# Two products side by side where TensorE first reads a fresh activation, in a two-layer hybrid diffusion block

## What is computed

```python
def reference(x, c, ctx, ...):
    for i in range(DEPTH):                      # DEPTH = 2
        sh1, sc1, g1, sh2, sc2, g2 = split(silu(c) @ ada_w[i] + ada_b[i], 6)
        h = modulate(rmsnorm(x, norm1_g[i]), sh1, sc1)
        # one input projection h @ w_in: SSD, short convolution, latent attention, Fourier, gates
        merged = sum(sigmoid(gate[k]) * (branch[k] @ w_branch[k]) for k in range(4))
        x = x + g1 * (merged @ w_out[i])
        h = modulate(rmsnorm(x, norm2_g[i]), sh2, sc2)
        x = x + g2 * (square(relu(h @ mlp_w1[i])) @ mlp_w2[i])
    return rmsnorm(x_latent, final_norm_g)
```

## Time and profile before

| what | us |
|---|---|
| median of 3 runs (lowest, highest) | 3272.09 (3267.53, 3280.63) |
| the profiled execution, first to last instruction | 3278.3 |
| TensorE matmul busy in it | 2998.9 (91%) |
| DVE, POOL, ACT busy in it | 1713.4 (52%), 875.8 (27%), 859.5 (26%) |
| TensorE idle, ended by `h_lo` on DVE | 66.3 in 23 waits |
| mean granted TensorE clock | 0.937 of full speed |

### The profile page before, as it was taken

One profiled execution on the slowest core, in us unless ns is written; L12 is line 12 of the kernel. 1 busy time (PEld: TensorE's weight loads), 2 busy tenths in 40 slices (PEclk: granted clock), 3 DMA queues, 4 the chain that ended last, 5 costly groups with the idle time before them and its releaser, 6 DMA issues. The chain is left out here.

```text
span 3278.3 us, 35493 instructions
## 1 busy us (share of the span) xinstructions
PE 2998.9 (91%) x14825; PEld 2420.8 (74%) x14825; DVE 1713.4 (52%) x1815; ACT 859.5 (26%) x1117; POOL 875.8 (27%) x412
## 2 busy tenths in 40 slices
PE   6898899999989899699999996889999988979998
PEld 5764588887878788578787885546877876768886
DVE  3464454543775575787777875641421664241123
ACT  1244311121122222212111222442222222332222
POOL 0210023321223222222222222202432242434442
PEclk6899999999997899899999998999999988989998
DMA  5400042331310033133333332102342201423331
GB/s 146 119 26 1 13 109 78 84 109 39 103 52 1 20 97 116 40 90 99 100 90 92 101 103 76 43 0 58 97 116 58 71 14 44 130 71 93 93 97 64
DMA packets 422264, 242.21 MB, mean 74 GB/s; under 512 B 20284, under 2 KB 418140, under 8 KB 421468
## 3 DMA queue, kind: packets, MB, share of 16 engines
q1 hardware_dynamic: 417388, 216.59, 24.1%
q10 hardware_dynamic: 4240, 23.27, 1.8%
q0 software_dynamic: 480, 0.10, 0.1%
HBM read 231.54 MB, written 8.39 MB: 73 GB/s over the span
## 5 line engine op out<-in xcount | busy, mean ns | idle before, releaser
L893 POOL TENSOR_TENSOR w_lo<-raw,w_hi 128x1024 fp32r<-128x1024 f32 x318 | 778.7, 2449 | 2233.7 <-ACT w_hi L915 2233.7
L426 PE MATMUL slot<-h_hi,w_hi 128*128 128x256 f32 (+1 forms) x2632 | 797.4, 361 | 67.2 <-DVE h_lo L1260 66.3
L426 PE MATMUL slot<-h_lo,w_hi 128*128 128x256 f32 (+1 forms) x2632 | 785.2, 357 | 0.0
L426 PE MATMUL slot<-h_hi,w_lo 128*128 128x256 f32 (+1 forms) x2632 | 784.6, 356 | 0.0
L426 PEld LDWEIGHTS slot<-h_hi,w_hi 128*128 128x128 f32 x2632 | 498.1, 192 | 154.4 <-issue 64.9
L915 ACT ACTIVATE w_hi<-raw 128x1024 fp32r<-128x1024 f32 x318 | 336.0, 1057 | 906.8 <-PE slot L426 532.5
L426 PEld LDWEIGHTS slot<-h_lo,w_hi 128*128 128x128 f32 x2632 | 505.4, 192 | 72.2 <-issue 0.5
L426 PEld LDWEIGHTS slot<-h_hi,w_lo 128*128 128x128 f32 x2632 | 504.3, 192 | 72.4
L1304 DVE TENSOR_REDUCE ksum<-prod 128x128 f32<-128x1024 f32 x160 | 318.9, 1993 | 5.5
L1257 DVE TENSOR_TENSOR prod<-raw,silc 128x1024 f32<-128x1024 f32 x160 | 278.0, 1738 | 2.8
L426 PE MATMUL slot<-f_hi,w_hi 128*128 128x512 f32 (+1 forms) x768 | 238.1, 364 | 16.2 <-DVE f_lo L1260 16.2
(11 more groups left out here) (254 smaller groups left out, 3328.9 us busy)
## 6 DMA issues: line engine op xcount, KB each, us to landing
raw<-in_w_in_dram SPq DMA_DIRECT2D x130, 512.0 KB, 3.9
raw<-in_mlp_w_dram SPq DMA_DIRECT2D x128, 512.0 KB, 4.0
raw<-in_ada_w_dram SPq DMA_DIRECT2D x96, 512.0 KB, 5.1
raw<-in_w_branch_dram SPq DMA_DIRECT2D x32, 512.0 KB, 3.5
raw<-in_w_out_dram SPq DMA_DIRECT2D x16, 512.0 KB, 3.7
x_spill<-x ACTq DMA_DIRECT2D x2, 3072.0 KB, 8.7
x<-x_spill ACTq DMA_DIRECT2D x2, 3072.0 KB, 10.8
dft<-in_dft_dram ACTq DMA_DIRECT2D x2, 2048.0 KB, 10.2
```

The lines of the kernel that those rows point to most:

```text
L426: last = pe.matmul(o[:, c0:c0 + nt], w[:, k, col:col + P], a[:, k, t0:t0 + nt], start=(k == rows[0] and n == 0), stop=(k == rows[-1] and n ...
L893: pool.tensor_tensor(w_lo[:, place[s] % 2, :], raw[:, s % NRAW, :], w_hi[:, place[s] % 2, :].bitcast(F32), ALU.subtract).then_inc(*does("w ...
```

## The change

A new function `product_pair` makes two products together. It takes two PSUM slots and waits for both weight tiles; then, for each contraction tile, it waits for the activation and issues the 6 (or 3) matmuls of the first product and those of the second. It replaces the first two products after each norm of a layer and at the output projection, six pairs in the whole kernel. In `w1` of layer 0 the two `ada_sum` of these products now stand behind the pair.

```diff
+            def product_pair(keys, a_hi, a_lo, sp, ready):
+
+                outs = [take(key) for key in keys]
+                both = [weights(key, key) for key in keys]
+                for k in range(KD):
+                    ready(k)
+                    for o, (wh, wl) in zip(outs, both):
+                        for n, (w, a) in enumerate(((wh, a_hi), (wh, a_lo), (wl, a_hi))):
+                            for c0, t0, nt in sp:
+                                last = pe.matmul(o[:, c0:c0 + nt], w[:, k, 0:P], a[:, k, t0:t0 + nt],
+                                                 start=(k == 0 and n == 0), stop=(k == KD - 1 and n == 2))
+                        if k == KD - 1:
+                            last.then_inc(slot_full, 1)
...
-                for f in range(2):
-                    product((L, "kva", f), (L, "kva", f), KD, 0, h_hi, h_lo, ALL,
-                            (lambda k: pe.wait_ge(*when("h_lo", (L, 1, k)))) if f == 0 else None)
+                product_pair([(L, "kva", f) for f in range(2)], h_hi, h_lo, ALL,
+                             lambda k: pe.wait_ge(*when("h_lo", (L, 1, k))))
...
-                for f in range(KD):
-                    product((L, "out", f), (L, "out", f), KD, 0, h_hi, h_lo, spans(L),
-                            (lambda k: pe.wait_ge(*when("merged_lo", (L, k)))) if f == 0 else None)
+                product_pair([(L, "out", f) for f in range(2)], h_hi, h_lo, spans(L),
+                             lambda k: pe.wait_ge(*when("merged_lo", (L, k))))
+                for f in range(2, KD):
+                    product((L, "out", f), (L, "out", f), KD, 0, h_hi, h_lo, spans(L))
                 mean_of_x((L, "ms", 2), spans(L))
                 for c in range(4):
-                    for f in range(KD):
-                        product((L, "w1", c, f), (L, "w1", c, f), KD, 0, h_hi, h_lo, spans(L),
-                                (lambda k: pe.wait_ge(*when("h_lo", (L, 2, k)))) if c == f == 0 else None)
+                    if c == 0:
+                        product_pair([(L, "w1", c, f) for f in range(2)], h_hi, h_lo, spans(L),
+                             lambda k: pe.wait_ge(*when("h_lo", (L, 2, k))))
+                        for f in range(2):
+                            ada_sum((L, "w1", c, f))
+                    for f in range(0 if c else 2, KD):
+                        product((L, "w1", c, f), (L, "w1", c, f), KD, 0, h_hi, h_lo, spans(L))
                         ada_sum((L, "w1", c, f))
```

## The result

The changed kernel took 3307.4 us (median of 4 runs, 3301.38 to 3315.7), the kernel before, run beside it, 3276.4 (4 runs, 3267.53 to 3284.57): 31 us more by the medians; the ratio is 1.0111 (36 us), 95% interval 1.0076 to 1.0145 (25 to 48 us). The same kernel run again later beside 29 runs of before: 3300.3 against 3271.5, 29 us more; 1.0080 (1.0056 to 1.0104, 18 to 34 us). The forecast was 25 us more and 3297, with a range of its own of 3288 to 3304 and a wide one of 3284 to 3308: the measured time lies above the first. The sign and the place of the loss held.

A forecast was written before the change was run, and what follows sets the result against it. TensorE, busy 91% of the span, was taken to bound the kernel. Six places summed to +20.2 us, three clock falls added 5.1: +25 us on the median, 3297 us, own range 3288 to 3304, wide range 3284 to 3308.

The forecast's parts named there:

- Where no time can be won: First waits for h_lo, where no activation step is ready: a pair waits the same; h_lo waits fall from 66.3 to near 48 us.
- The late tile of out 1: Output projections: pairs wait for the second weight tile, rounded behind eight copies of `merged`; waits of 12 and 9 us.
- place 2: Output projection of layer 0: third product starts 11.4 us later, from 8.3 late start, 2.9 refill gap and rounding.
- place 5: Output projection of layer 1: late tile, half-clock start and refill make the third product start 11.0 us later.
- rival B: Whole kernel: clock stays up at all gaps, short half-clock starts, faster w_lo at `out`; +16 us, 3288, chance 0.13.
- The refill gap: Behind every pair but `w1` of layer 0, TensorE waits a weight refill less one step: 2.9 to 3.7 us.
- The sums of w1: `w1` of layer 0: second sum waits 9.3 us for DVE; with a half-clock start of 2.3, plus 1.9 us.
- What kva gives back: `kva`: the third product starts earlier, by 0.5 us in layer 0 and 4.8 us in layer 1.
- The clock, the step that failed: Five refill gaps: half-clock restarts cost between 0 and 8.6 us; three falls taken, 5.1 us.
- Rival C: Refill gaps: clock falls at all five and stays down 5.85 us, 2.9 each; +35 us, 3307, chance 0.08.
- The base: Whole kernel: the 25 us were added to the median of three runs of before, giving 3297 us.
- A (tile there in time, -14): Output projections and refills: `out 1` does not delay the pair and refills hide; about -14 us, 3258, chance 0.03.

The follow-up runs named there:

- early: The changed kernel, but ACT rounds the weight tile of `out 1` ahead of the eight copies of `merged`: 3286.0 us, ratio 1.0045 to before.
- lead1: The changed kernel with the second product of all six pairs starting one step after the first: 3285.2 us beside 3289.0 for before, one run each.
- lead3: Kernel before with pairs only at `kva` (both layers) and `w1` of layer 1, second product three steps after the first: 3261.0 us, ratio 0.9972.
- Fill: The changed kernel with useless matmuls on constants in the waits for `out 1` and in the refill gaps: 3281.5 us, ratio 1.0040 to before.
- out_only: The changed kernel with `kva` and `w1` put back, pairs only at the output projections: 3298.0 us, ratio 1.0084 to before.
- no_out: The changed kernel with the output projections put back, pairs only at `kva` and `w1`: 3274.4 us, ratio 1.0007 to before.

## Why the prediction was right in kind and short in size

**Where no time can be won.** The four first waits stayed at 47.6 us (forecast near 48). Right.

**The late tile of out 1.** Forecast waits of 12 and 9 us, measured 11.96 and 8.78. From the start of the wait to the third product, place 2 grew by 10.5 (forecast 11.4) and place 5 by 11.5 (11.0). Early shows the cause: with the rounding ahead of the copies the waits are h_lo's again. POOL took 4.29 us for that tile beside DVE's work, as before, and 2.83 in layer 1 (2.85 before), so the gain that rival B gave it did not come.

**The refill gap.** Forecast 2.9 in layer 0, 3.26 and 3.7 in layer 1; measured 2.69, 2.69, 2.66, 3.06 and 3.47. 0.2 us less each; the step was right and its unit a little large. Lead1 and lead3 confirm the form of the term. The Trainium skill, "Perfetto Trace Analysis", section Optimization Strategy, says that an equal, repeated gap can mean too few buffers, and the trace agrees: five gaps of 2.66 to 3.47 us behind pairs that hold both weight places; lead3 adds that with the same two buffers another order of the same matmuls removes it too.

**The sums of w1.** 9.3 us of waiting forecast, 9.04 measured; the place, with its half-clock start, +1.9 forecast, +2.0 measured.

**What kva gives back.** From the first matmul to the start of the third product, layer 1: -4.8, measured -4.4; layer 0: -0.5, measured -0.8 (in before the third product started at 125.50, not at 125.34, since a step there takes 1.06 us). But these starts are at half clock, so of the 4.4 only 2.8 remain at the end of place D, and of the 0.8 nothing: to the first copy of `kr` it is +0.4. The -0.1 of A in the table comes from a first h_lo that was 0.5 us earlier in that execution.

**The clock, the step that failed.** I wrote "I take three falls, 5.1". In the first trace there were five. By (1 - PEclk) x 7.5 in the windows above they cost 1.4, 1.4, 1.6, 3.0 and 1.7: 9.1 us, not 5.1. With the measured starts of the third products (-0.8 + 10.5 - 4.4 + 11.5 + 0.4, and 2.0 for place 3, together 19.2) that makes 28.3, as in the table; with a noise of some 2 us in the table, so close a match is luck. Still, the sum without the falls was right to 1 us, and the term for the falls was 4 us too small; it passed even the 8.6 us that I had named as the most. In the second execution the clock fell at four of the five gaps and at the fifth (layer 0, output projection) not, and the four cost 1.5, 3.1, 3.0 and 1.7, so 9.3 us. The largest miss is place 5; windows of after and before over its products 3 to 8:

```profile
2858.49:2900.86 42.37, 37.79 (x146) 29.46 (x146) 11.30 (x13) 10.87 (x13) 18.19 (x7) 0.90 0.34 96
```

```profile
2844.02:2882.78 38.76, 34.18 (x147) 27.14 (x145) 12.05 (x14) 12.45 (x15) 18.42 (x7) 0.99 0.31 87
```

The same matmuls take 3.6 us more at 0.90 than at 0.99.

Why three? I had chosen the number by the nearness of 2.9 to 3.58, as if the trace of before had no other wait in that region, and that was wrong. It has twelve waits of 2.44 to 4.02 us that TensorE enters at full clock, the 3.58 among them, and in the 7.5 us behind every one of them the granted clock was 0.80 or less. Two of them, with the windows behind them:

```profile
187.58 0.59 PE L426 MATMUL slot<-ln_hi,w_hi 128*128 128x256 f32 x2 [2.96 <-DVE ln_lo L1260]
1908.95 0.78 PE L426 MATMUL slot<-f_hi,w_hi 128*128 128x256 f32 x2 [2.56 <-DVE f_lo L1260]
```

```profile
187.58:195.08 7.50, 7.50 (x34) 6.46 (x35) 1.73 (x3) 1.14 (x2) 3.41 (x1) 0.77 0.24 70
1908.95:1916.45 7.50, 7.50 (x36) 6.53 (x37) 4.38 (x5) 1.91 (x2) 2.34 (x1) 0.77 0.24 61
```

So five falls at about 1.7 us, 8.6, could have been read from before: 20.2 + 8.6 is 29, which is what was measured. The wait of 2.26 us, behind which I had seen no fall, was one case: in lead3 the clock fell behind the same wait in the same place,

```profile
2807.88 0.77 PE L426 MATMUL slot<-h_hi,w_hi 128*128 128x512 f32 x1 [2.26 <-DVE h_lo L1285]
```

with 0.77 us where the earlier trace rows has 0.47. Rival C had the count right and the price too high (2.9 each for 1.8): its +35 is 6 to 7 us above the 28.3 and 29, my 25 is 3 to 4 below. Its 3307 equals the first measured median by luck, since before was on the high side beside it. Fill shows that this is the clock and not the waits: the same late tiles, the clock held up, 12.1 us less.

The Trainium skill, "TensorE: Matmul & The Clock Gate", section Loop structure matters more than you think, sets dense matmul work against waits between groups. The prediction weighed it on both sides, and here the bad side won. The pair kept the clock up inside itself: 0.85 over the pair of `w1` in layer 0 (1349.92 to 1369.35), where the first product alone had 0.69 in before (1345.25 to 1363.36). It lost it at all five gaps behind.

**The base.** I added to the median of three runs, 3272.1. Medians of before in the later comparisons were 3276.4, 3269.6 and 3271.5, so that was sound to some 4 us; the 3307.4 stands on a comparison in which before was on the high side. Of the 10 us between 3297 and 3307.4, then, 4 are the base, 3 to 4 the falls, and the rest is within the scatter of the runs.

**The rivals.** A (tile there in time, -14) fell: its point of decision was whether the tile of `out 1` is ready by the time of the first h_lo, and it was not by 8 us. Even early, which makes it ready, is +14.7, because the refill gaps remain and the first h_lo comes later. A wanted both, and lead3 is what comes nearest. B (+16) fell with the clock at the gaps.

## What to carry to other kernels

Interleaving two accumulation groups holds all their operand buffers to the end of both, so count the buffers first: in this kernel the gap behind was the refill less the work that was left when the first buffer came free, and running the second group three steps behind the first removed it at `kva` (2.7 us) and left 1.5 us of 3.5 at `w1` of layer 1. The pair also starts when the later of its operands is there, so it belongs only where both are ready before the shared fresh one; here that was the norms and not the output projection. Where an order on one engine is changed, look at what then runs side by side: in early the first `h_lo` tripled beside POOL's w_lo. And add to each new wait on TensorE, if it is as long as those here (2.4 to 3.5 us), the half-clock restart as likely, not as possible, and count what the clock did behind all waits of that length in the trace that is there, not behind the nearest one.

## What the runs showed of the hardware that I had not expected

Of twelve gaps of 2.66 to 2.70 us behind pairs of layer 0's size, in after, its second run, out_only, no_out and early, ten were followed by half clock; the other two stood both behind the pair of the output projection of layer 0 (granted clock 1.00 in the 7.5 us after), where in two more executions it fell. In lead1 the gaps of 1.66, 1.68, 1.66 and 2.79 us were followed by 1.00, that of 2.37 by 0.77. Over all eleven traces, TensorE entered 141 waits of 2.4 to 4.1 us at full clock, and behind 131 of them the clock was below full in the next 7.5 us; of the ten others the longest was 2.96. So the same wait in the same place can cost 0 or 1.4 us and more, and the length of the wait alone doesn't decide it. What does stays open.

Where DVE's `h_lo` and POOL's w_lo of the output projection of layer 0 ran side by side, one of them was long: in before POOL's took 4.36 us (2.40 elsewhere) and DVE's stayed at 0.95, in early the first of DVE's took 3.12 and POOL's 3.17. What decides which of them pays isn't shown.

The unchanged SSD stretch took 1098 to 1115 us in eleven executions, 1114.3 beside a granted clock of 0.76 in the part shown above and 1103.8 beside 0.85. The 16 us between the ends are more than half of what this change costs, which is why one pair of spans could not have measured it.
